# Second mixer of a two-block transformer kernel: seven of eight rotary blocks finished by adding DMA transfers from GpSimd's queue, with a new table of steps

## The reference

```python
def apply_rope(x, cos, sin):
    x1, x2 = jnp.split(x, 2, axis=-1)
    ...
    return jnp.concatenate([x1 * c - x2 * s, x2 * c + x1 * s], axis=-1)

def diff_mixer(h, w_in, lam, subln_g, w_out, cos, sin, lambda_init):
    proj = jnp.einsum('btd,de->bte', h, w_in)
    q, k, v = jnp.split(proj, 3, axis=-1)
    q = apply_rope(q.reshape(bsz, T, C_HEADS * 2, HEAD_DIM), cos, sin)...
    k = apply_rope(k.reshape(bsz, T, C_HEADS * 2, HEAD_DIM), cos, sin)...
    ...
        s = jnp.einsum('bqhcd,bshcd->bhcqs', qb, k) * scale
        p = masked_softmax(s, key_pos[None, :] <= tq[:, None])
        a = p[:, :, 0] - lam_val * p[:, :, 1]
        return jnp.einsum('bhqs,bshe->bqhe', a.astype(v.dtype), v)
    ...
    o = rms_norm(o, subln_g) * (1.0 - lambda_init)
    return jnp.einsum('bte,ed->btd', o.reshape(bsz, T, ODD_MIX), w_out)
```

## Time and profile before

| | |
|---|---|
| median of 3 runs | 1143.5 us (1143.5 to 1143.5) |
| profiled execution | 1144.46 us, of which the span from first to last instruction is 1142.7 us |
| mean granted TensorE clock | 0.995 |
| busy in the span | PE 1119.2 us, DVE 831.1, ACT 587.0, POOL 56.8 |
| the second mixer in the trace | about 338 to 457 us |

### The profile page before, as it was taken

One profiled execution on the slowest core, in us unless ns is written; L12 is line 12 of the kernel. 1 busy time (PEld: TensorE's weight loads), 2 busy tenths in 40 slices (PEclk: granted clock), 3 DMA queues, 4 the chain that ended last, 5 costly groups with the idle time before them and its releaser, 6 DMA issues.

```text
span 1142.7 us, 15900 instructions
## 1 busy us (share of the span) xinstructions
PE 1119.2 (98%) x6253; PEld 929.6 (81%) x6253; DVE 831.1 (73%) x1368; ACT 587.0 (51%) x912; POOL 56.8 (5%) x105
## 2 busy tenths in 40 slices
PE   8999999999999999999999999999999998999997
PEld 7767568888878887888888878888879886888886
DVE  6569449878775777698788889877884557656664
ACT  7345445454445675645444674444466566544442
POOL 1101000000000000010000001000011000000000
PEclk9999999999999999999999999999999999999999
DMA  9526259987844334798876279778636443755530
GB/s 337 169 93 226 76 211 369 340 294 274 309 155 147 122 137 165 268 400 310 297 281 239 74 259 408 287 280 301 237 121 230 157 149 98 276 200 199 185 111 37
DMA packets 39578, 252.19 MB, mean 221 GB/s; under 512 B 6744, under 2 KB 6944, under 8 KB 10832
## 3 DMA queue, kind: packets, MB, share of 16 engines
q1 hardware_dynamic: 26928, 189.67, 46.3%
q0 software_dynamic: 12576, 61.51, 14.8%
HBM read 249.37 MB, written 4.25 MB: 222 GB/s over the span
## 4 chain that ended last, share of the span: by engine, by line
PE 87%; DVE 7%; ACT 3%; issue 1%; DMA 1%; POOL 0%; DVEq 0%; ACTq 0%
PE bank L1487 51%; PE bank L1638 25%; PE bank L1931 2%; PE bank L1690 2%; PE bank L1715 1%; PE bank L1753 1%; PE bank L1571 1%; DVE x L922 1%; PE bank L1912 1%; DMA u<-qk 1%; DVE work L920 1%; PE bank L2002 1%; DVE wlo L1051 1%; DVE wlo L899 1%; DVE us L966 0%
## 5 line engine op out<-in xcount | busy, mean ns | idle before, releaser
L899 DVE TENSOR_TENSOR wlo<-raw,whi 128x2048 fp32r<-128x2048 f32 x140 | 319.0, 2283 | 61.2 <-ACT whi L554 61.1
L554 ACT ACTIVATE whi<-raw 128x2048 fp32r<-128x2048 f32 x141 | 267.9, 1904 | 2.4 <-DMA raw<-in_stream 1.5
L1487 PE MATMUL bank<-whi,hh 128*128 128x512 f32 x544 | 214.1, 394 | 0.0
L1487 PE MATMUL bank<-wlo,hh 128*128 128x512 f32 x544 | 212.4, 390 | 0.0
L1487 PE MATMUL bank<-whi,hl 128*128 128x512 f32 x544 | 211.8, 389 | 0.0
L1638 PE MATMUL bank<-us,whi 128*128 128x512 f32 x832 | 197.0, 389 | 0.0
L1638 PEld LDWEIGHTS bank<-us,whi 128*128 128x128 f32 x832 | 156.2, 188 | 32.4
L1487 PE MATMUL bank<-us,whi 128*128 128x256 f32 x880 | 168.0, 291 | 0.0
L1487 PEld LDWEIGHTS bank<-us,whi 128*128 128x128 f32 x880 | 137.7, 192 | 9.0 <-issue 8.2
L1487 PE MATMUL bank<-whi,us 128*128 128x512 f32 (+2 forms) x384 | 122.2, 386 | 5.7 <-DVE us L966 1.6
L625 ACT ACTIVATE hh<-work 128x512 fp32r<-128x512 f32 x56 | 35.4, 633 | 173.3 <-PE bank L1487 173.3
(11 more groups left out here) (239 smaller groups left out, 1172.5 us busy)
## 6 DMA issues: line engine op xcount, KB each, us to landing
raw<-in_stream SPq DMA_DIRECT2D x176, 1024.0 KB, 4.9
qk<-in_w_mod POOLq DMA_DIRECT2D x48, 1024.0 KB, 5.6
bias_rows<-bias_heads POOLq DMA_DIRECT2D x4, 768.0 KB, 17.6
u<-bias_rows POOLq DMA_DIRECT2D x16, 128.0 KB, 2.9
vo<-feature_rows POOLq DMA_DIRECT2D x3, 512.0 KB, 8.8
raw<-in_stream SPq DMA_DIRECT2D x2, 696.0 KB, 8.0
x<-in_x SPq DMA_DIRECT2D x2, 512.0 KB, 4.7
cb<-feature_rows POOLq DMA_DIRECT2D x2, 512.0 KB, 6.6
```

The source lines that it names most:

```text
L554: nc.scalar.activation(whi[:, c % RING, 0:w], raw[:, n % RING, 0:w], ACT.Copy).then_inc(hi_ready, 1)
L899: nc.vector.tensor_tensor(wlo[:, c % RING, 0:w], raw[:, raw_index(c) % RING, 0:w], whi[:, c % RING, 0:w].bitcast(fp32), ALU.subtract).then ...
L1487: ins = mm(out, st, mv, start=start and i == 0, stop=stop and i == 2, skip_group_check=True)
```

## The change

For the rotations r = 0 to 6, DVE writes the cosine product into `qk` itself and no longer into the bank. When both products are done (`d_t2`), POOL issues four transfers from `work` to `qk` that add to what stands there, one for each 32 partitions, from each half of a head to the other (`rotate`). They count `d_rot[r % 2]` by 16 each, 64 for a rotation. Scores wait for `d_rot` instead of `d_add`; projections that reuse a bank wait for `d_t2`, since the bank is free when DVE has read it. DVE's rotation r waits for rotation r - 2's transfers, which read the same half of `work`. Rotation 7 keeps the swap on PE and the copy on ACT. POOL has the transfers in its queue behind the sixteen loads of its first group (m = 0) and ahead of its wait for the end of the mixer. All three tables have new numbers.

```diff
-D_PE = {"score": {0: (4, 2), 1: (5, 0), 2: (6, 2), 3: (8, 0), 4: (8, 3), 5: (9, 1), 6: (12, 2), 7: (13, 0)},
+D_PE = {"score": {0: (5, 1), 1: (5, 1), 2: (7, 2), 3: (8, 2), 4: (8, 2), 5: (8, 2), 6: (12, 2), 7: (12, 2)},
...
+            def rotate(r):
+
+                j = FEATURES[r]
+                pool.wait_ge(d_t2, r + 1)
+                for s in range(4):
+                    here, there = slice(32 * s, 32 * s + 32), slice(32 * (s ^ 1), 32 * (s ^ 1) + 32)
+                    pool.dma_start(qk[there, 2 * j:2 * j + 2, :],
+                                   work[here, 2 + r % 2, :].rearrange("p (b n) -> p b n", b=2),
+                                   accum_op=ALU.add).then_inc(d_rot[r % 2], 16)
...
                 elif m == 1:
+                    for r in range(7):
+                        rotate(r)
                     pool.wait_ge(used, LAST_OF[3] + 1)
...
-                if q == 1 and 1 <= i <= 12 and MIXER[i - 1][0] == "f":
+                if (i, q) == (12, 1):
                     _, j, k = MIXER[i - 1]
-                    r = FEATURES.index(j)
-                    act.wait_ge(d_sw, r + 1)
+                    act.wait_ge(d_sw, 1)
...
                     if r >= 2:
-                        dve.wait_ge(d_sw, r - 1)
-                    rope_in_place(bank[k], j < 4, r).then_inc(d_t2, 1)
+                        dve.wait_ge(d_rot[r % 2], 64 * (r // 2))
+                    rope_in_place(bank[k], j < 4, r, out=None if r == 7 else qk[:, 2 * j:2 * j + 2, :]).then_inc(d_t2, 1)
...
-                    pe.wait_ge(d_add if ph == "d" else b_copied, 2 * (p // 2) + 2)
+                    if ph == "b":
+                        pe.wait_ge(b_copied, 2 * (p // 2) + 2)
+                    else:
+                        pe.wait_ge(d_rot[0], 64 * (p // 2 + 1))
+                        pe.wait_ge(*((d_add, 1) if p >= 6 else (d_rot[1], 64 * (p // 2 + 1))))
                 if p:
                     pe.wait_ge(s_max[ph], 2 * p)
...
             def dswap(i, q):
-                if q == 1 and i <= 12 and MIXER[i - 1][0] == "f":
+                if (i, q) == (12, 1):
```

More of the change, by code:

```diff
@@ L94 @@
 FEATURES = tuple(j for kind, j, _ in MIXER if kind == "f")
-D_PE = {"score": {0: (4, 2), 1: (5, 0), 2: (6, 2), 3: (8, 0), 4: (8, 3), 5: (9, 1), 6: (12, 2), 7: (13, 0)},
[L100 to L112, removed]
+D_PE = {"score": {0: (5, 1), 1: (5, 1), 2: (7, 2), 3: (8, 2), 4: (8, 2), 5: (8, 2), 6: (12, 2), 7: (12, 2)},
+        "turn": {0: (6, 2), 1: (6, 3), 2: (8, 2), 3: (9, 0), 4: (9, 3), 5: (10, 3), 6: (13, 2), 7: (13, 3)},
+        "value": {0: (7, 0), 1: (7, 0), 2: (9, 0), 3: (9, 1), 4: (11, 1), 5: (11, 1), 6: (13, 3), 7: (14, 0)},
+        "out": {0: (8, 1), 1: (10, 2), 2: (12, 0), 3: (14, 3)}}
@@ new lines @@
+D_ACT = {"exps": {0: (5, 1), 1: (6, 0), 2: (7, 0), 3: (8, 0), 4: (9, 0), 5: (9, 2), 6: (13, 1), 7: (13, 1)},
+        "copy": {0: (6, 1), 1: (6, 2), 2: (7, 3), 3: (9, 0), 4: (10, 0), 5: (11, 1), 6: (13, 2), 7: (13, 3)},
+        "upper": {0: (7, 1), 1: (10, 2), 2: (13, 0), 3: (14, 2)},
+        "square": {0: (6, 2), 1: (9, 1), 2: (11, 3), 3: (14, 0)},
+        "root": {0: (6, 3), 1: (9, 3), 2: (11, 3), 3: (14, 1)}}
+D_DVE = {"max": {0: (5, 1), 1: (5, 1), 2: (7, 0), 3: (8, 0), 4: (8, 3), 5: (8, 3), 6: (12, 2), 7: (12, 3)},
+        "lower": {0: (8, 1), 1: (10, 3), 2: (12, 3), 3: (15, 1)},
+        "join": {0: (5, 2), 1: (6, 0), 2: (7, 3), 3: (8, 2), 4: (9, 1), 5: (10, 2), 6: (13, 0), 7: (13, 3)},
+        "mean": {0: (7, 0), 1: (9, 2), 2: (11, 2), 3: (14, 2)},
+        "scale": {0: (7, 1), 1: (10, 1), 2: (11, 2), 3: (15, 0)}}
@@ L338, in build @@
         d_t2, d_sw, d_add, d_v = sem("d_t2"), sem("d_sw"), sem("d_add"), sem("d_v")
+        d_rot = [sem(f"d_rot{i}") for i in range(2)]
         v_ps, b_v = sem("v_ps"), sem("b_v")
@@ L1103, in pair_lower, with rope_in_place @@
                     .then_inc(ol_ready, 1)
-            def rope_in_place(b, q, r, n=2):
+            def rope_in_place(b, q, r, n=2, out=None):
                 cs = con[:, (C_COSQ if q else C_COS):][:, 0:T].unsqueeze(1).to_broadcast([128, n, T])
@@ L1111, in rope_in_place @@
                 link(nc.vector.tensor_tensor(t2, src, sn, ALU.mult))
-                return nc.vector.tensor_tensor(src, src, cs, ALU.mult)
+                return nc.vector.tensor_tensor(src if out is None else out, src, cs, ALU.mult)
             nc.vector.memset(one, 1.0).then_inc(col_ready, 1)
@@ L1792, in steps @@
                     elif c == 0 and q < 3:
-                        pe.wait_ge(d_add if ph == "d" else b_copied, 7 + q // 2)
+                        pe.wait_ge(*((b_copied, 7 + q // 2) if ph == "b" else (d_add, 1) if q else (d_t2, 7)))
                 for c in range(3):
@@ L2013, in _ @@
                     if k == 0:
-                        pe.wait_ge(d_add, 5)
+                        pe.wait_ge(d_t2, 5)
                     rows_of_values(DIFF + i, k, steps)
@@ L2021, in _ @@
                     elif i > 2:
-                        pe.wait_ge(d_add, {5: 1, 6: 3, 7: 4, 11: 6}[i])
+                        pe.wait_ge(d_t2, {5: 1, 6: 3, 7: 4, 11: 6}[i])
                     features(DIFF + i, bank[k], steps=steps if i > 2 else None).then_inc(used, 1)
```

## The result

The changed kernel took 1148.72 us in the median of 5 runs (1147.31 to 1149.63), the kernel before 1143.5 us (1139.22 to 1143.5) beside it: a ratio of 1.0055, 95% interval 1.0036 to 1.0074. It is slower, where no change that can be told was forecast; 1148.72 lies inside the range.

The account below looks back on a forecast made before the run. PE, busy 98% of the span, was taken to bound the kernel. -6.65 + 4.2 + 3.6 + 1.0 - 0.6 = +1.55 us on the median 1143.5 gave 1145.0 us, range 1141.0 to 1149.5.

Parts of the forecast that it names:

- The swaps: Second mixer, PE: seven swaps removed, 2 of 1.20 and 5 of 0.85 us, 6.65 us off PE.
- Scores back to back: Second mixer: scores 1, 5 and 7 each wait 1.4 us on PE for the previous pair's maxima, 4.2 us.
- Score 4's wait: PE at score 4 waits 3.6 us for rotation 5's transfers, landing taken as 2.4 us; bounds 3.1 and 5.8.
- The bound of 4.6: Upper landing time for rotation 5's transfers, from the row under a stream load; score 4 would then wait 5.8 us.
- Score 0: Score 0 leaves 3.9 us for rotation 1's last transfer to land, so its wait costs nothing.
- The clock: After score 4's wait, 3.4 us at the lower 1.2 GHz clock cost PE 1.0 us; bounds 0 and 1.7.
- The end: Last lower part placed before two halves of wlo, so PE's final wait shrinks: 0.6 us back, bounds 0 and 0.9.
- slower: Rival: adding transfers land late, from 3.2 us on over 2.3 us slower; 1147.1 or 1150.1 us; chance 0.41.

Follow-up runs that it names:

- spread: Changed kernel with load 60 held, scores 1, 4, 5 and 7 later, score 3, join 5 and scale 1 earlier: 1135.6 us, ratio 0.9928 to 0.997 against before.
- transfers alone: Changed kernel's seven adding transfers with the three step tables of the kernel before: 1143.8 us, ratio 1.0012 to 1.0035 against the kernel before.
- scores 4 and 5 later: Changed kernel with scores 4 and 5 placed at (9,1) and (9,3), their following steps moved behind them: 1143.5 us, ratio 1.0005 to 1.0039 against before.
- spread, turn 2 later: The spread kernel with turn 2 one quarter later on PE, at (8,3): 1139.2 us, ratio 0.9954 to 0.9994 against the kernel before.

## Why the prediction was wrong, point by point

**The swaps.** Right: -6.65 us was forecast. In the two mixers whose clock stayed up, what is left when the waits are taken off is -6.3 for seven swaps (spread) and -3.4 for four (3.75 had been expected). The -7.6 of the changed kernel is a remainder that also holds the error of the clock's term.

**Scores back to back.** Right: 4.2 us forecast, 1.35 + 1.35 + 1.38 = 4.1 measured.

**Score 4's wait.** The chain was right up to the transfers. Against the end of unit 7 (395.69 us): rope at 2.5 (forecast 2.45), last issue at 5.7 (5.6), PE at score 4 at 4.6 (4.4). The landing was mis-sized: "I take 2.4 us" stood for 3.9, so the wait was 5.1 instead of 3.6. That is the step that failed first. The 2.4 lay between rows of copies; a quiet add takes 1.4 us longer than a quiet copy (3.3 against 1.9), and load 63 put 0.6 on top. The two are not simply added: with that load in flight the last plain copy takes 3.1 us too. The bound of 4.6 held.

**Score 0.** The step that failed next: "3.9 us for the landing, enough by every quiet row." It was enough for a quiet add (3.3), not for one that a load crosses (6.2). The load came there because the new tables take the maxima of pair 0 out from between two halves of wlo. DVE frees the buffer earlier and SP issues load 60 at 365.4; with the old tables it issues it at 372.2. DVE's rows of the kernel with the old tables (transfers alone), the two halves with the maxima between them:
```profile
362.82 1.22 DVE L1063 TENSOR_TENSOR wlo<-raw,whi 128x1024 fp32r<-128x1024 f32 x1
369.84 0.29 DVE L1090 CUSTOM_DVE_ANT_0 P<-bank,con 128x128 f32<-128x128 f32 x1 [5.80 <-PE bank L1706]
...
370.96 1.22 DVE L1063 TENSOR_TENSOR wlo<-raw,whi 128x1024 fp32r<-128x1024 f32 x1
```
I had followed SP's loads for rotation 5 and not for rotation 1. 2.4 us were missing here.

**The clock.** One slow stretch of 3.4 us was counted, losing 1.0; there were two of 6.8, losing 5.3. The largest miss, 4.3 us: one of the two came with the wait at score 0 that I had missed, and both were twice as long as the earlier trace rows showed. The 5.3 takes half of PE's busy time as lost; with the swaps at the -6.3 of the spread kernel, 4.0 us are left for the clock and the miss is 3.0, still the largest.

**The end.** Right: 0.6 forecast, 0.6 measured.

Together: 1.5 + 2.4 + 4.3 is 8.2; less 0.9 for the swaps' remainder and 0.1 for the scores back to back, that is the 7.2 us between 1.55 and 8.75. The rival *slower*, that the transfers land late, is the one that happened; it had the wait at score 0 and not the clock behind it. On the median the miss is smaller, 1148.7 against 1145.0: the kernel before had 3 us of its own to lose in the first mixer, in its profiled execution at least. The kernel before's medians beside the experiments are 1140.7 to 1141.3 us, against which the changed kernel's 1148.7 would be 7 to 8 us slower (across comparisons), nearer the mixer's 8.75. That 1148.7 lies in the range is luck: the upper end stood for transfers that land in 5.4 us, and what the sum lacked was mostly the clock and score 0.

## What to carry to other kernels

Place a step for the landing of what it waits for beside the loads that the new order brings, and follow every queue that the move speeds up: a load issued half a microsecond later delayed these transfers by 3 us. On a PE that is otherwise full, count with a half-clock stretch at waits like those at scores 0 and 4 here (2.4 to 5.2 us): in the changed kernel each cost 2 to 2.7 us, about as much again as the shorter of its two waits. A copy's landing is no price for an adding transfer.

## What the runs showed of the hardware

- An adding transfer of 64 KB from SBUF to SBUF lands 2.5 to 3.3 us after issue, four in a row and no load near, where a plain copy of the same bytes lands in 1.8 to 1.9. POOL's issues begin 0.5 us apart with either. A 1 MB load issued half a microsecond behind a set of adding transfers held its last one to 6.2 us; a plain copy in the same place took 2.0.
- At each wait of 2.4 to 5.2 us at scores 0 and 4 of the kernels with transfers the clock fell to 0.50, for 6.8 or 10.2 us, where the earlier trace rows show 3.4. Length alone does not decide: 2.44 us at score 0 (scores 4 and 5 later) brought such a stretch, 2.45 at turn 3 (spread, turn 2 later) none. What does was not settled.
- Runs of the kernel before differ by up to 8 us. The traces show half-clock stretches in unchanged parts, from 3.4 us in the kernel before (from 53.4 and from 640.4 us) and in the changed one (from 657.8) to 10.2 us in spread (from 632.5); spread, turn 2 later has none there, and its span is 2.6 us shorter than spread's though its mixer is 1.4 longer. That such stretches make up all of the 8 us is not shown. The mixer by itself was the better measure.
